# First attention: product with V in per-step parts, last three chunks rotated beside the heads, output projection begun on the first group's tiles

## What is computed

```python
h = rms_norm(x, norm_mix_pre)
qa, ka, va, qb, kb, vb = split(h @ w_in)          # 8 + 2 + 2 + 8 + 2 + 2 heads of 64
qa = rope(rms_norm(qa per head)); ka = rope(rms_norm(ka per head))
out_a = softmax(qa ka^T / 8) va                   # all 512 keys; 4 query heads share a kv head
qb = rope(qb); kb = rope(kb)
out_b = softmax with a sink(qb kb^T / 8) vb       # keys within 128 positions
mixed = concat(rms_norm(out_a), rms_norm(out_b)) @ w_out
x = x + rms_norm(mixed)
```

## Time and profile before

| | before |
|---|---|
| median of 3 runs | 1495.15 us |
| profiled execution | 1496.76 us |
| its span, first to last instruction | 1495.0 us |
| mean granted TensorE clock | 0.969 |
| busy: TensorE / VectorE / ScalarE / GpSimd | 94% / 45% / 36% / 10% |
| chain that ended last: TensorE / VectorE / ScalarE | 85% / 8% / 3% |

### The profile page before, as it was taken

One profiled execution on the slowest core, in us unless ns is written; L12 is line 12 of the kernel. 1 busy time (PEld: TensorE's weight loads), 2 busy tenths in 40 slices (PEclk: granted clock), 3 DMA queues, 4 the chain that ended last, 5 costly groups with the idle time before them and its releaser, 6 DMA issues.

```text
span 1495.0 us, 14898 instructions
## 1 busy us (share of the span) xinstructions
PE 1403.6 (94%) x6182; PEld 1107.5 (74%) x6182; DVE 678.9 (45%) x893; ACT 539.5 (36%) x717; POOL 147.1 (10%) x132
## 2 busy tenths in 40 slices
PE   6696998898999999999899999999999999999996
PEld 5464465686888888887688777678888888888874
DVE  5576545345444444222633453356364444333345
ACT  5335654444233232223322444454332233232232
POOL 3352010222000000100200000001100000000012
PEclk9798998899999999999899999999999999999997
DMA  5110000121232232333122110213223232223321
GB/s 223 56 57 29 1 1 1 57 85 57 85 100 98 88 109 78 97 97 116 51 105 85 57 57 32 76 69 113 85 85 113 85 109 89 76 96 97 105 78 57
DMA packets 20291, 117.76 MB, mean 79 GB/s; under 512 B 2432, under 2 KB 3072, under 8 KB 9472
## 3 DMA queue, kind: packets, MB, share of 16 engines
q1 hardware_dynamic: 19088, 114.57, 22.3%
q10 hardware_dynamic: 1136, 2.24, 0.4%
HBM read 114.70 MB, written 2.10 MB: 78 GB/s over the span
## 4 chain that ended last, share of the span: by engine, by line
PE 85%; DVE 8%; ACT 3%; issue 2%; DMA 1%; POOL 1%; POOLq 0%; DVEq 0%; SPq 0%; ACTq 0%
PE ps L420 83%; DVE rt L1109 1%; DVE nmax L1258 1%; ACT w_hi L748 1%; PE ps L584 1%; DMA w_raw<-weights 1%; DVE prob L1106 1%; DVE w_lo L1102 1%; DVE y L1102 1%; DVE X L1102 0%; ACT rt L748 0%; DVE ps L1109 0%; POOL sqsum L364 0%; DVE OUT L1109 0%; DVE h_lo L1109 0%
## 5 line engine op out<-in xcount | busy, mean ns | idle before, releaser
L420 PE MATMUL ps<-h_hi,w_hi 128*128 128x512 f32 x1248 | 499.5, 400 | 30.5 <-DVE w_lo L1102 13.8
L420 PE MATMUL ps<-h_lo,w_hi 128*128 128x512 f32 x1248 | 490.4, 393 | 0.0
L420 PE MATMUL ps<-h_hi,w_lo 128*128 128x512 f32 x1248 | 490.2, 393 | 0.0
L1102 DVE TENSOR_TENSOR w_lo<-w_raw,w_hi 128x2048 fp32r<-128x2048 f32 (+2 forms) x116 | 243.0, 2097 | 283.8 <-ACT w_hi L748 283.7
L420 PEld LDWEIGHTS ps<-h_hi,w_hi 128*128 128x128 f32 x1248 | 237.3, 190 | 89.0 <-issue 20.4
L420 PEld LDWEIGHTS ps<-h_lo,w_hi 128*128 128x128 f32 x1248 | 237.4, 190 | 51.4 <-issue 3.2
L420 PEld LDWEIGHTS ps<-h_hi,w_lo 128*128 128x128 f32 x1248 | 237.1, 190 | 50.6
L748 ACT ACTIVATE w_hi<-w_raw 128x2048 fp32r<-128x2048 f32 (+2 forms) x116 | 201.5, 1738 | 194.2 <-DMA w_raw<-weights 193.9
L364 POOL TENSOR_TENSOR sqsum<-sqsum,sq 128x512 f32<-128x512 f32 x62 | 92.6, 1493 | 962.3 <-ACT sq L748 960.7
L420 PE MATMUL ps<-mid_hi,w_hi 128*128 128x512 f32 x352 | 136.9, 389 | 0.0
L420 PE MATMUL ps<-mid_lo,w_hi 128*128 128x512 f32 x352 | 136.9, 389 | 0.0
(11 more groups left out here) (155 smaller groups left out, 1231.6 us busy)
## 6 DMA issues: line engine op xcount, KB each, us to landing
w_raw<-weights SPq DMA_DIRECT2D x82, 1024.0 KB, 4.8
w_raw<-weights SPq DMA_DIRECT2D x32, 704.0 KB, 4.1
X<-x_t SPq DMA_DIRECT2D x4, 512.0 KB, 9.7
out_t<-OUT SPq DMA_DIRECT2D x8, 256.0 KB, 2.0
c<-constants ACTq DMA_DIRECT2D x1, 1280.0 KB, 8.6
wp_raw<-weights SPq DMA_DIRECT2D x1, 1024.0 KB, 4.6
hf<-p_t ACTq DMA_DIRECT2D x1, 512.0 KB, 3.7
w_raw<-weights SPq DMA_DIRECT2D x2, 128.0 KB, 2.3
```

What stands on the lines that cost most here:

```text
L420: return nc.tensor.matmul(out, lhsT, rhs, start=start, stop=stop, skip_group_check=loose)
L1102: return nc.vector.tensor_tensor(out, a, b, op)
```

## The change

- `ORDER1` swaps chunks so that the queries A come earlier (j = 5 is chunk 2, j = 7 chunk 3). The last three chunks (j = 9, 10, 11, from `LATE1` = 9: queries 8 and 9, values B) are still projected in `in1` but evacuated to buffers of their own (`hf`, `sq`). Their rotation or transposition on TensorE is issued in steps 1, 5 and 9 of the loop, their ropes on VectorE behind steps 3 and 7, their copies on ScalarE in steps 5, 9 and 12. GpSimd's order keeps its sequence.
- On ScalarE the split of a unit at odd j >= 3 stands first instead of behind the square and `high_qk`.
- The loop no longer waits for all ropes: the first scores wait for the evacuation of their banks, each second head of group A for its own chunk.
- `weighted(g)` is issued as four parts of two matmuls, one in each of the steps 4g + 6 to 4g + 9, between the scores and the transposes. `copy_out` moves from s % 8 == 4 to s % 8 == 6, norm A from step 38 to step 40.
- `out1` begins with two units (four groups) k slice by k slice, before the norm of group B is known: `total` of B stands ahead of slice 1, its `factor` ahead of slice 2. ScalarE splits unit 8 and the matrix `wp` before the first evacuation of `out1`, the other splits behind odd groups.
- `prob` now lies in `F`'s memory, and so does the scratch of the late ropes, because the rope tables must live on.

```diff
-NORM_A_STEP = 38
+NORM_A_STEP = 40
...
-ORDER1 = [5, 4, 0, 10, 1, 6, 2, 7, 3, 8, 9, 11]
+ORDER1 = [5, 4, 0, 10, 1, 2, 6, 3, 7, 8, 9, 11]
+LATE1 = 9
...
+        prob, rt_late = F[:, 4:7, :], F[:, 0:2, :]
...
-                prob = sb("prob", [P, 3, S], stack=st2)
...
+        y_late = [hf[:, 0, :], hf[:, 1, :], sq[:, 0, :]]
+
+        def y_of(j):
+            return y[:, j % 3, :] if j < LATE1 else y_late[j - LATE1]
+
+        def rot_bank(j):
+            return 4 + j % 2 if j < LATE1 else 7 if j != 10 else 6
+
+        def roped_upto(j):
+            return sum(c not in V1 for c in ORDER1[:j + 1])
...
-            def first_units(phase, u, units, ks, hi, lo, readies, before_last=None):
+            def first_units(phase, u, units, ks, hi, lo, readies, before={}):
 
                 for n, (k, ready) in enumerate(zip(ks, readies)):
-                    if before_last is not None and n == len(ks) - 1:
-                        before_last()
+                    if n in before:
+                        before[n]()
...
+            LATE_STEPS = {1: 9, 5: 10, 9: 11}
...
-            item(11)
-
-
-            pe.wait_ge(roped, len(ROPED))
-            pe.wait_ge(rope_done, ROPED.index(NORMED[-1]) + 1)
             pe.wait_ge(v_ready, 1)
-            pe.wait_ge(evac_dve, EVAC["in1", 11][1])
 
             def scores(s):
...
                 if s >= 3:
                     pe.wait_ge(exp_done, s - 2)
+                else:
+                    pe.wait_ge(evac_dve, EVAC["in1", 8 + s][1])
+                if s < 32 and s % 8 == 0:
+                    pe.wait_ge(rope_done, roped_upto(ORDER1.index(h // 2)))
...
-            def weighted(g):
+            def weighted(g, n):
...
-                if c >= 2 and g % 2 == 0:
-                    pe.wait_ge(ot_ready, c - 1)
...
-                pe.wait_ge(pt_ready, 4 * (g + 1))
+                if n == 0:
+                    if c >= 2 and g % 2 == 0:
+                        pe.wait_ge(ot_ready, c - 1)
+                    pe.wait_ge(pt_ready, 4 * (g + 1))
...
-                for n, (kb, q0, q1) in enumerate(order):
-                    last = mm(ps[r:r + HD, 5 + c % 2, q0 * P:q1 * P], v[:, kb, kv * HD:(kv + 1) * HD],
-                              PT[:, g % 2, kb, q0 * P:q1 * P], n == 0, n == len(order) - 1, loose=True)
-                last.then_inc(av_done, 1)
+                kb, q0, q1 = order[n]
+                part = mm(ps[r:r + HD, 5 + c % 2, q0 * P:q1 * P], v[:, kb, kv * HD:(kv + 1) * HD],
+                          PT[:, g % 2, kb, q0 * P:q1 * P], n == 0, n == len(order) - 1, loose=True)
+                if n == len(order) - 1:
+                    part.then_inc(av_done, 1)
...
                 scores(s + 2)
+                if s >= 6:
+                    weighted((s - 6) // 4, (s - 6) % 4)
+                if s in LATE_STEPS:
+                    item(LATE_STEPS[s])
                 pe.wait_ge(pn_ready, s + 1)
...
-                if s % 4 == 2 and s > 2:
-                    weighted(s // 4 - 1)
...
-            weighted(15)
-            pe.wait_ge(ot_ready, 8)
-            pe.wait_ge(pt_ready, 64)
-            total(n_group_b)
-            factor(n_group_b)
-
-
-            first_units("out1", U_OUT1, 1, KS, h_hi, h_lo,
-                        [nm.lo(k + 1) for nm in (n_group_a, n_group_b) for k in range(4)])
-            for u in range(1, UNITS_OUT1):
+            for n in range(2, 4):
+                weighted(14, n)
+            for n in range(4):
+                weighted(15, n)
+
+
+            def total_group_b():
+                pe.wait_ge(ot_ready, 8)
+                total(n_group_b)
+
+            first_units("out1", U_OUT1, 2, KS, h_hi, h_lo,
+                        [nm.lo(k + 1) for nm in (n_group_a, n_group_b) for k in range(4)],
+                        {1: total_group_b, 2: lambda: factor(n_group_b)})
+            for u in range(2, UNITS_OUT1):
...
             for j in range(12):
                 c = ORDER1[j]
+                if j in (3, 5, 7, 9):
+                    split(j // 2 + 2)
...
-                high_qk(j - 2)
-                if j % 2 and j < 11:
-                    split(j // 2 + 2)
-                if j:
+                if j - 2 < LATE1:
+                    high_qk(j - 2)
+                if j == 1:
+                    split(2)
+                if 0 < j <= LATE1:
                     finish(j - 1)
-            high_qk(10)
-            finish(11)
...
-                if s % 8 == 4 and s > 8:
-                    copy_out(s // 8 - 1)
+                if s % 8 == 6 and s > 8:
+                    copy_out((s - 14) // 8)
+                if s in (5, 9):
+                    high_qk(9 if s == 5 else 10)
+                if s == 12:
+                    finish(11)
...
+            split(U_OUT1 + 2)
+            act.wait_ge(wp_landed, 16)
+            af(wp_hi[:, :], wp_raw[:, :], ACT.Copy).then_inc(wp_hi_ready, 1)
             for j in range(KD):
...
-                if j % 2 == 0:
-                    split(U_OUT1 + j // 2 + 2)
-                if j == 1:
-                    act.wait_ge(wp_landed, 16)
-                    af(wp_hi[:, :], wp_raw[:, :], ACT.Copy).then_inc(wp_hi_ready, 1)
+                if j in (1, 3, 5):
+                    split(U_OUT1 + j // 2 + 3)
...
                 dve.wait_ge(group_done, GROUP["in1", j])
-                if j >= 3:
+                if 3 <= j < LATE1:
...
                 evacuate(j)
...
-                if j:
+                if 0 < j <= LATE1:
                     rope(j - 1)
...
                 negmax(s + 2)
+                if s in (3, 7):
+                    rope(9 if s == 3 else 10)
```

More of the change, by code:

```diff
@@ L153, in build @@
             sb("c1_head", [P, C_COSA - C1_AT], stack=st)
-            with ExitStack() as st2:
-                prob = sb("prob", [P, 3, S], stack=st2)
             sb("c1_tables", [P, 4 * S], stack=st)
@@ L391, in low_qk @@
                     rows, other = slice(HD * i, HD * i + HD), slice(HD * (1 - i), HD * (1 - i) + HD)
-                    t = y[rows, j % 3, :]
+                    t = y_of(j)[rows, :]
                     if c in (4, 10):
@@ L500, in item @@
                 c = ORDER1[j]
-                free_item(j - 2)
+                if j < LATE1:
+                    free_item(j - 2)
+                elif j == 10:
+                    free_item(LATE1 - 1)
+                else:
+                    free_item({LATE1: LATE1 - 2, 11: LATE1}[j])
                 if j == 0:
@@ L523, in beside @@
                     factor(n_mix_pre)
-                for i in {3: (0,), 4: (1, 2), 5: (3, 4)}.get(j, (j - 1,) if j > 5 else ()):
+                for i in {3: (0,), 4: (1, 2), 5: (3, 4)}.get(j, (j - 1,) if 5 < j <= LATE1 else ()):
                     item(i)
@@ L615, in ffn @@
                 if wide:
-                    first_units(phase, u_ff, 2, KS, h_hi, h_lo, parts_of(nm.lo), lambda: total(nm))
+                    first_units(phase, u_ff, 2, KS, h_hi, h_lo, parts_of(nm.lo), {KD - 1: lambda: total(nm)})
                     factor(nm)
@@ L649, in vee @@
                 last.then_inc(v2tr_done, 1)
-            first_units("in2", U_IN2, 2, KS, h_hi, h_lo, parts_of(n_mix2.lo), lambda: total(n_mix2))
+            first_units("in2", U_IN2, 2, KS, h_hi, h_lo, parts_of(n_mix2.lo), {KD - 1: lambda: total(n_mix2)})
             factor(n_mix2)
@@ L831, in high_qk @@
                     if c in (4, 10):
-                        af((KA if c == 4 else KB)[HD * (1 - i):HD * (1 - i) + HD, 0, i, :], y[rows, j % 3, :],
+                        af((KA if c == 4 else KB)[HD * (1 - i):HD * (1 - i) + HD, 0, i, :], y_of(j)[rows, :],
                            ACT.Copy)
-                    af(dst, y[rows, j % 3, :], ACT.Copy).then_inc(roped_hi, 1)
+                    af(dst, y_of(j)[rows, :], ACT.Copy).then_inc(roped_hi, 1)
             act.wait_ge(c0_landed, 32)
@@ L845, in _ @@
                     if j >= 2:
-                        act.wait_ge(roped, sum(o not in V1 for o in ORDER1[:j - 1]))
+                        act.wait_ge(roped, roped_upto(j - 2))
                     af(ysq[:, j % 2, :], y[:, j % 3, :], ACT.Square).then_inc(ysq_ready, 1)
-                high_qk(j - 2)
-                if j % 2 and j < 11:
-                    split(j // 2 + 2)
-                if j:
+                if j - 2 < LATE1:
[3 more added lines that the diff above has]
+                if 0 < j <= LATE1:
                     finish(j - 1)
-            high_qk(10)
-            finish(11)
             split(UNITS_IN1 + 1)
@@ L862, in copy_pt @@
                 if s == 0:
-                    act.wait_ge(rope_done, len(ROPED))
+                    act.wait_ge(rope_done, roped_upto(LATE1 - 1))
                 if g >= 2 and s % 4 == 0:
@@ L1207, in evacuate @@
                         dve.wait_ge(rope_done, ROPED.index(ORDER1[j - 3]) + 1)
-                scaled(ps[:, j % 4, :], y[:, j % 3, :]).then_inc(evac_dve, 1)
+                scaled(ps[:, j % 4, :], y_of(j)).then_inc(evac_dve, 1)
             def rope(j):
```

(11 more changed lines are left out.)

13 lines of the change are left out of this document (9 added, 4 removed).

## The result

The changed kernel takes 1463.62 us (median of 4 runs, 1462.92 to 1464.36), the kernel before 1496.03 on the same chip (4 runs). The ratio is 0.9785, 95% interval [0.977, 0.98]: 32.4 us faster, where 48.8 were forecast.

The account below looks back on a forecast made before the run. TensorE was taken as the bound (94% busy), gains only from its holes and low clock before the first output projection's end. 18.8 + 10.0 + 11.2 + 8.8 = 48.8 us off gave 1446.4 us; range 1436 to 1466.

Parts of the forecast that it names:

- rival A: Loop: the switch is not hidden, 0.2 us in some 57 steps, 1455; with GpSimd's slow halves 1463; chance 0.20.
- the switch: TensorE in the loop: going between transposes or scores and a product with V; taken as 0.04 us a step, bounds 0 and 0.2.
- GpSimd's slow halves: Input projection: GpSimd's low halves of keys taking 3.23 us instead of 1.29, delaying evacuations; 8 us.
- Part 3: Loop, first half: product with V in quarters, 1.80 us a step for 25 steps; steps 0 to 31 10.0 us shorter.
- Part 2: First-head steps of the loop: late ropes and slowed VectorE operations add 1.6 and 1.0 us, 8.5 becoming 11.1.
- Part 1: Input projection: new orders and late chunks bring the first nmax at 111.7 instead of 130.5, 18.8 us off.
- the lower bound of 11 us off: Input projection: gain if all GpSimd low halves under a rope or w_lo are the long kind, 11 us instead of 18.8.
- Part 4: Loop, second half: heads of group B at 6.2 us, norm A at full clock; 59.2 instead of 70.45, 11.2 us off.
- the 1.0 us of stall allowed: Loop, second half: the share of VectorE's 7 us of norm work let show as delay, 1.0 us.
- Part 5: Output projection: first k slices cover norm B's sum, total and factor; 46.3 instead of 55.1 us, 8.8 off.
- Rival B: Loop: the parts bring nothing, it stays bound by the chain over VectorE and ScalarE; 1467.6 us; chance 0.10.
- Rival C: Loop: TensorE stays at 1.2 GHz between parts and waits, so slower, up to 1559 us; chance 0.02.

Follow-up runs that it names:

- e9: Changed kernel with 128 weight columns in each product with V, a head's 64 and 64 zeros, output still correct: 1455.81 us, ratio 0.9723.
- e3: Changed kernel with all 128 columns of V as weights in each product with V, output not the attention's: 1458.0 us (one run).
- e6: Changed kernel with ropes of chunks 9 and 10 moved to steps 7 and 11, and unit 7's rounding into the loop: 1459.71 us, ratio 0.9753.
- e12: The changed kernel as it is, measured again on the last chip: 1464.03 us (5 runs), ratio 0.978; its profile is of the slowest run.
- e11: Changed kernel with GpSimd writing zeros into the low halves of keys A and B instead of subtracting: 1460.7 us (one run).
- e8: Changed kernel with the old chunk order and ScalarE's splits behind the copies again, late chunks still late: 1470.05 us, ratio 0.9829.
- e4: Changed kernel with the output projection as before, both norms first, then one unit k slice by k slice: 1471.93 us, ratio 0.9841.
- e1: Changed kernel with a head's product with V as one block of eight matmuls again: 1474.32 us, ratio 0.9854.
- e5: Changed kernel with each step's part of the product with V behind the transposes, not ahead of them: 1478.01 us, ratio 0.9875.
- e10: Changed kernel with the edits of e9 and e6 together: 1446.27 us, ratio 0.9669.

## Why the prediction was right, and which step failed

The time fell, and 1463.62 lies in the range given, 2.4 us inside its upper end: what came is the band of rival A (1453 to 1464), not the forecast's. Rival A had the switch right, 9 us over what was taken, and 8.6 came. Its other 8 us, GpSimd's slow halves, did not come as it said; smaller misses in Parts 1 to 5 and the 2.2 us between profiles and medians made up as much, and that the sum ends at A's 1463 is luck.

- **Part 3, the term for the switch, failed.** It read "behind 512-column scores a load has a long matmul to hide under, so I take 0.04". It measured 0.30 us a step (2.055 against 1.755). Over 25 steps of the first half that is 6.4 us more than the 1.80 taken, and in the second half it is 3.5 us (61.9 against 58.4 in e9, most steps 0.19 apart) where 1.3 were in the sum. The upper bound, 0.2, was too low as well: it came from one side of the switch, the 0.18 in front of a block, and the way out of the block was never priced. e3 and e9 show the cause: weights of 64 columns among weights of 128.
- **The rule that was weighed** ("TensorE: Matmul & The Clock Gate", part 3, "The mechanism", of the Trainium skill) pulls a weight load ahead for other row groups or the background buffer. All loads here take all 128 rows. With 128 columns the step is 1.755 us and the load stands ahead of its matmul, with 64 the load starts after the running matmul: the trace agrees with the rule's second half for wide weights and has a case of the same rows where it doesn't happen. Width is not in the rule.
- **Part 2 was too small:** 12.8 us instead of 11.1. The late rope costs what was taken: TensorE waits 2.00 us for the scaling behind it. What the sum had not is the clock behind that wait: steps 4 and 5 are 1.6 us longer than in e6, at 0.72 and 0.67. In e12 the same six steps take 13.7.
- **Part 3's rest:** step 6 to step 31 took 52.3 us, of which 25 x 2.055 explain 51.4. The last 0.9 are three steps: 2.37 us with a wait for rope 10, 2.55 with the four transposes of chunk 11 (0.49), and 2.28 at the end with group B's scores over 384 keys, their mask and sink. With 1.7 and 6.4 they make the 9.0 us missing in this half.
- **Part 1 was 3.1 us late** (first nmax 114.8, forecast 111.7, inside the 109 to 116 given). GpSimd's halves were costed by what they take themselves; what they do to VectorE was left out. e11 shows it: without the subtractions the first nmax is at 110.9. The Trainium skill, "SBUF — State Buffer", section "Who interferes with whom", has VectorE and GpSimd contending, and the trace agrees: VectorE's 0.69 become 1.67 while GpSimd's halves are 1.62 instead of 1.29. Its stronger outcome, the lower bound of 11 us off, didn't come: 15.6 did. e8 confirms that the orders of ScalarE and of the chunks do their part (7.4 us).
- **Part 4** gave 8.7 of 11.2, and the switch makes 2.2 of the 2.5 missing; the waits of TensorE for VectorE in this half fell to one of 0.8 us, so the 1.0 us of stall allowed was about right. That its products run "at full clock throughout" came true in this execution, and not in that of e12.
- **Part 5** gave 8.5 of 8.8, and e4 gives it back (8.3).
- **Rival B** (parts bring nothing) is out: e1 costs 10.7 us. **Rival C** is out as a whole: the clock is 1.00 from 129.9 to 250. But the steps stand at 2.055 us, outside the 1.76 to 1.9 named, and one sign of being wrong came, a clock under 0.9 in the loop (0.87 in the first steps, 0.83 at norm A in e12); each cost about 1.5 us.

## What to carry to other kernels

When matmuls of different kinds are interleaved, add up the distances between starts across every kind of switch, in and out; weights of 64 columns between weights of 128 cost 0.30 us a visit of two 512-column matmuls here, and padding them with zeros to 128 gave 7.8 us. Where an engine sets the pace, cost the neighbours of its instructions too, not only the instructions: rope 9 at its worst place costs its full 1.9 us, and four steps later 0.3. Where a part of a product frees a buffer, its place among the work that waits for that buffer has to be measured: behind the transposes instead of ahead of them, the gain of spreading was lost (14.4 us in e5), and only some 2.3 of it by the wait that one would have looked for. Before a difference of one or two us between two profiles is explained, compare the granted clock in both, and a second profile of the same kernel.

## What the runs showed of the hardware

A load of 64-column float32 weights was not taken ahead of a running matmul with 128-column weights, a load of 128 columns was; a product with the narrow weights took 0.10 us more on the way in, 0.145 on the way out and 0.055 behind the following transposes (differences of 0.64, 1.00, 0.41 to 0.545, 0.855, 0.355).

VectorE's two-input operation on 128x512 float32 takes 0.69 us with GpSimd idle and up to 1.67 beside GpSimd's two-input subtraction, but not always: some beside it are hardly longer (0.84, 0.87). Beside GpSimd's memset in e11 the first operation of the normed rope takes 0.74, beside the subtraction 1.16.

TensorE's clock in the stretch around norm A differed between executions of nearly the same loop, and between two of the same kernel (1.00 in the first profile of the changed kernel, 0.83 from 210 to 220 in e12). Two stretches of e3:

```profile
176.25:197.00 20.75, 20.64 (x125) 15.66 (x124) 13.11 (x35) 13.98 (x41) 3.84 (x3) 1.00 0.00 1
197.00:217.00 20.00, 19.88 (x109) 16.03 (x107) 12.00 (x39) 10.19 (x31) 0.53 (x1) 0.83 0.00 0
```

The engine was busy in all but 0.1 us of each, and the granted clock fell from 1.00 to a mean of 0.83. e6 has the same (0.84 from 198 to 220, 21.93 of 22.00 busy, after 1.00 with no hole at all), and its second half is 3.1 us longer than the changed kernel's, whose first profile kept 1.00 there (203 to 224) with 20.89 of 21.00 busy; e9 and e10 kept 1.00 as well. By these profiles a fall here costs 1.5 us (e12) to about 3 (e3, e6), and no wait of TensorE stands ahead of it. What the engine did before it is the same each time: in e1 to e6, e8 and e12 the first slow matmuls come at the end of the sixteen one-column matmuls of norm A's `total` or within some 2 us behind them. But the first profile of the changed kernel, e9, e10 and e11 have the same sixteen and no fall. What brings it about was not settled; it is as large as the difference that e6 was to show.
